# Prompt attention of a hybrid decoder step: rows of logits in a ring of six banks, one bank each for turned probabilities and values, and TensorE's program reordered

## The chip, the cores and the metric

The kernel runs on one core of a Trainium2 chip. The metric is the device time of one execution in microseconds (us), taken as the median of several executions.

## The reference, cut to what matters

One inference step of a one-layer decoder: RMSNorm, a combined input projection, a state-space branch, a sparse-attention branch, gates, an output projection and an MLP, for a prompt of 1024 positions and for 8 samples of 4 new tokens each. The change touches only the attention of the prompt, after its top-k mask is known:

```python
def attend_selected(q, k_sel, v_sel, sel_idx, q_pos, rel_bias):
    dist = q_pos[None, :, None] - sel_idx
    valid = dist >= 0
    bias = rel_bias.astype(jnp.float32)[t5_bucket(dist)]
    logits = jnp.einsum('bthd,btkhd->bthk', q, k_sel).astype(jnp.float32) * HEAD_DIM ** -0.5
    logits = logits + jnp.swapaxes(bias, -1, -2)
    logits = jnp.where(valid[:, :, None, :], logits, -jnp.inf)
    p = jax.nn.softmax(logits, axis=-1)
    return jnp.einsum('bthk,btkhd->bthd', p.astype(v_sel.dtype), v_sel)
```

There are 8 heads of 64 channels, 1024 prompt positions, and up to 256 keys selected for a position. The kernel does not gather the selected keys: it computes all logits up to the diagonal and hides the keys that were not selected with a mask.

## The kernel before, in words

The kernel is written by hand, engine by engine, in a row of blocks with a barrier between them; every wait is a semaphore. The block of the change is the prompt attention, whose engine programs start at line 1738 (SyncE) and 1766 (TensorE). Before it stand the projections, the indexer and the selection; after it come the attention of the samples, the output projection and the MLP.

**Tiles and pairs.** The prompt is cut into 8 tiles of 128 queries (i = 0 to 7). Tile i looks at `keys_of(i)` = 128 (i + 1) keys. Within a tile the heads go two at a time: pair u stands for (i, m), heads 2m and 2m + 1, called hh = 0 and 1. There are 32 pairs, and everything runs over them in order.

**What one pair costs on TensorE** (all in `@block.tensor`, from line 1766):
- *logits* (line 1781): q times k in fp32, 64 channels deep, so the two heads use the two row halves of the array at once; up to 512 keys go into one PSUM bank, so tiles 4 to 7 need two banks a head. Then the mask is added by a bf16 matmul (line 1787; tiles 0 and 1 only add the triangle, line 1789), and `qk_done` goes up for each head.
- *transposes* (line 1805): the probabilities (128 queries x 128 keys each) are turned, up to four into one bank. Such a set of up to four is a *group* (`groups`, `p_groups`); a head of tiles 4 to 7 has two of them.
- *values* (line 1823): for each block of 128 keys and each head one matmul of 64 columns, the two heads side by side in the column halves of the array, summed in the tile's values bank.
- *inverses* (line 1835), once a tile: the reciprocals of the row sums, spread over the channels, are turned so that they can multiply the result.

**The other engines.** VectorE adds the relative bias to the nearest 256 keys of a row in PSUM (line 1862) and takes the row's maximum (line 1867), in `row_max`; copies the turned groups of head 1 to SBUF (line 1876); forms the reciprocals (`invert`, lines 1882 and 1886); and multiplies the finished values by the turned reciprocals (`finish`, line 1892). ScalarE copies the turned groups of head 0 (line 1916), copies the turned reciprocals (`take_inverses`, line 1923) and computes the exponentials of a row from PSUM to SBUF with their sum (line 1932, each followed by the read of its accumulator). The copies go to a ring of 8 slots in SBUF (`PTs`). GpSimd and SyncE only prepare the next block: 32 small loads of bias, the value rows and pages of the samples' caches.

**The eight PSUM banks.** Banks 0 to 3 hold rows of logits (`row_bank`, line 1713): in tiles 0 to 3 one bank a row, so two pairs at a time; in tiles 4 to 7 two banks a row, so one pair. Banks 4 and 5 take the turned groups in turn (group g goes to bank 4 + g % 2, and waits until the copy of group g - 2 is done: `bank_free`). Banks 6 and 7 hold the values of an even and an odd tile.

**The order.** TensorE's program is a list written out by hand:

```python
            logits(0)
            for u, (i, m) in enumerate(PAIRS):
                if u + 1 < NPAIR:
                    logits(u + 1)
                transposes(u)
                if m == 1 and i:
                    inverses(i - 1)
                if u:
                    values(u - 1)
```

So each iteration u issues the logits of the next pair, turns the probabilities of this one and multiplies the values of the last. `logits(u)` waits, in tiles 4 to 7, for both exponentials of the pair before (its banks), in the others for those of two pairs before. VectorE's order is row_max(u + 1), at a new tile invert(i - 1), the copies of pair u, and in the third pair of a tile finish(i - 1). ScalarE's is the copies of pair u, in the second pair take_inverses(i - 1), then the exponentials of pair u + 1.

## Time and profile before

| | |
|---|---|
| median of 3 runs | 1810.75 us |
| lowest and highest | 1806.47 and 1811.78 us |
| span of the profiled execution | 1809.0 us |
| TensorE busy, share of the span | 1655.9 us, 92% |
| VectorE, ScalarE, GpSimd busy | 1153.2, 740.1, 704.3 us |
| attention block of the prompt | 681.2 to 845.0 us of the span |

The profile is one execution. Its page gives the span, from the first to the last instruction, and not that execution's own time; the span is 1.75 us under the median of the runs. Engine names in the rows: PE is TensorE's matmuls, PEld its weight loads, DVE VectorE, ACT ScalarE, POOL GpSimd, SP SyncE; L1805 is line 1805 of the kernel. A row of the order in time gives the start in us of the span, the time to the end of the last instruction merged in it, the engine, line and operation, out<-in with shapes, how many instructions it merges, and in brackets how long the engine had been idle and what released it. One fp32 matmul of products or values is recorded as two, and the two heads' matmuls start together. Ends of matmuls are modelled, so the text reckons from start to start. PEclk is the clock granted to TensorE: 1.00 is 2.4 GHz, 0.50 is 1.2 GHz.

### The profile page before, as it was taken

To read this page: it belongs to the slowest core of one execution; us is meant where nothing else is said; L and a number is where in the kernel's file an instruction comes from. 1 tells how busy PE (TensorE), PEld (TensorE's weight loads), DVE (VectorE), ACT (ScalarE), POOL (GpSimd) and SP (SyncE) were. 2 spreads that over 40 slices of the span, in tenths; PEclk is the share of its full clock that TensorE was granted. 3 is DMA by queue.
4 is the path that set the end of the run, shared out by engine and by line. 5 is a ranking of instruction groups with operands and counts; after the bars stand their busy time and mean duration, and the time that the engine had idled before them with its cause. 6 is when DMAs were issued, how large, how long until landed. Compare 5 with 4: busy or idle time off the path is not lost.

```text
span 1809.0 us, 31521 instructions
## 1 busy us (share of the span) xinstructions
PE 1655.9 (92%) x12434; PEld 1526.2 (84%) x12448; DVE 1153.2 (64%) x1860; ACT 740.1 (41%) x1337; POOL 704.3 (39%) x435
## 2 busy tenths in 40 slices
PE   6899869978999998788799999899999989999998
PEld 6798539978999875555399998899999989999998
DVE  5772557999866537655244138765555579989786
ACT  6323446556433525443322334534444433333342
POOL 7021105875211100000444431344444477777782
PEclk9999989998999998999899999999999989999999
DMA  6322161212853105002562443454544365444432
GB/s 159 114 64 48 28 77 51 91 60 87 148 123 122 54 19 189 1 1 75 172 216 96 125 125 95 146 192 142 176 152 143 143 243 167 155 155 143 138 90 97
DMA packets 170199, 209.13 MB, mean 116 GB/s; under 512 B 27411, under 2 KB 114419, under 8 KB 170003
## 3 DMA queue, kind: packets, MB, share of 16 engines
q1 hardware_dynamic: 170050, 207.10, 38.0%
q8 instruction: 99, 1.62, 0.4%
q14 instruction: 50, 0.40, 0.1%
HBM read 148.28 MB, written 58.78 MB: 114 GB/s over the span
## 4 chain that ended last, share of the span: by engine, by line
PE 29%; POOL 9%; DVE 4%; DMA 3%; issue 2%; ACT 2%; SPq 1%; DVEq 0%; ACTq 0%; POOLq 0%
PE psum L139 9%; PE psum L141 9%; PE psum L140 9%; POOL da_lo L3140 5%; DMA view_at<-hid_dram 3%; POOL view_at L3156 1%; POOL view_at L3149 1%; ACT da_hi L3016 1%; POOL view_at L3159 1%; POOL view_at L3152 1%; DVE view_at L3220 1%; SPq L2602 1%; DVE b_lo L3226 1%; DVE view_at L3351 0%; PE psum L2741 0%
## 5 line engine op out<-in xcount | busy, mean ns | idle before, releaser
L139 PE MATMUL psum<-db_hi,da_hi 128*128 128x264 f32 x896 | 257.0, 287 | 15.4 <-DVE view_at L3336 8.1
L139 PE MATMUL psum<-b_hi,ua_hi 128*128 128x264 f32 x896 | 256.4, 286 | 11.0 <-DVE psum L3284 3.8
L141 PE MATMUL psum<-db_hi,da_lo 128*128 128x264 f32 x896 | 256.6, 286 | 0.0
L140 PE MATMUL psum<-db_lo,da_hi 128*128 128x264 f32 x896 | 256.6, 286 | 0.0
L141 PE MATMUL psum<-b_hi,ua_lo 128*128 128x264 f32 x896 | 255.2, 285 | 0.0
L140 PE MATMUL psum<-b_lo,ua_hi 128*128 128x264 f32 x896 | 254.8, 284 | 0.0
L139 PE MATMUL psum<-h_hi,w_hi 128*128 128x352 f32 x600 | 198.4, 331 | 20.8 <-POOL w_lo L211 20.8
L3136 POOL TENSOR_TENSOR ua_lo<-view_at,ua_hi 128x512 fp32r<-128x512 f32 x99 | 137.3, 1391 | 189.1 <-ACT ua_hi L2945 189.0
L211 POOL TENSOR_TENSOR w_lo<-view_at,w_hi 128x2048 fp32r<-128x2048 f32 (+1 forms) x18 | 82.3, 4570 | 296.4 <-ACT w_hi L205 296.3
L140 PE MATMUL psum<-h_lo,w_hi 128*128 128x352 f32 x600 | 195.7, 326 | 0.0
L141 PE MATMUL psum<-h_hi,w_lo 128*128 128x352 f32 x600 | 195.5, 326 | 0.0
L139 PEld LDWEIGHTS psum<-db_hi,da_hi 128*128 128x128 f32 x896 | 170.4, 190 | 17.7 <-issue 8.3
L3140 POOL TENSOR_TENSOR da_lo<-view_at,da_hi 128x1024 fp32r<-128x1024 f32 x56 | 148.3, 2667 | 93.6 <-ACT da_hi L3016 93.6
L139 PEld LDWEIGHTS psum<-b_hi,ua_hi 128*128 128x128 f32 x896 | 169.2, 189 | 12.5 <-issue 11.5
L140 PEld LDWEIGHTS psum<-db_lo,da_hi 128*128 128x128 f32 x896 | 169.6, 189 | 0.0
L141 PEld LDWEIGHTS psum<-db_hi,da_lo 128*128 128x128 f32 x896 | 169.6, 189 | 0.0
L141 PEld LDWEIGHTS psum<-b_hi,ua_lo 128*128 128x128 f32 x896 | 169.4, 189 | 0.0
L140 PEld LDWEIGHTS psum<-b_lo,ua_hi 128*128 128x128 f32 x896 | 169.3, 189 | 0.0
L3351 DVE TENSOR_TENSOR view_at<-psum,view_at 128x528 f32<-128x528 f32 x204 | 134.6, 697 | 25.9 <-PE psum L141 23.4
L3315 DVE TENSOR_TENSOR db_lo<-view_at,db_hi 128x1056 fp32r<-128x1056 f32 x56 | 127.6, 2278 | 24.2 <-ACT db_hi L3011 24.0
L139 PEld LDWEIGHTS psum<-h_hi,w_hi 128*128 128x128 f32 x600 | 115.5, 193 | 23.0 <-issue 21.3
L139 PE MATMUL psum<-w_hi,h_hi 128*128 128x256 f32 x432 | 127.1, 294 | 3.0 <-PEq L1048 2.3
(394 smaller groups left out, 4061.6 us busy)
## 6 DMA issues: line engine op xcount, KB each, us to landing
hid_dram<-view_at SPq DMA_DIRECT2D x112, 264.0 KB, 2.3
view_at<-hid_dram SPq DMA_DIRECT2D x56, 528.0 KB, 3.8
view_at<-w_in SPq DMA_DIRECT2D x18, 1024.0 KB, 5.5
view_at<-w_up SPq DMA_DIRECT2D x16, 1024.0 KB, 6.0
view_at<-w_down SPq DMA_DIRECT2D x32, 512.0 KB, 5.6
gate_dram<-view_at SPq DMA_DIRECT2D x48, 176.0 KB, 2.0
view_at<-gate_dram SPq DMA_DIRECT2D x16, 528.0 KB, 4.5
view_at<-cache_k SPq DMA_DIRECT2D x32, 256.0 KB, 3.0
```

Of the source, the lines that this page charges most:

```text
L139: nc.tensor.matmul(out, lhs[0], rhs[0], start=start, stop=False, skip_group_check=more)
L140: nc.tensor.matmul(out, lhs[0], rhs[1], start=False, stop=False, skip_group_check=more)
L141: return nc.tensor.matmul(out, lhs[1], rhs[0], start=False, stop=stop, skip_group_check=more)
L211: nc.gpsimd.tensor_tensor(w_low[n % 2][:, :, 0:width], w_raw[n % 2][:, :, 0:width], f32(w_high[n % 2][:, :, 0:width]), ALU.subtract).then_ ...
L2602: sp.dma_start(raw_d[d % 2][:, k0::2, cols], w_dn[d][:, k0::2, cols]).then_inc(raw_d_in[j], 16)
L3016: nc.scalar.activation(dah[n % SLOTS], src_d(n), ACT.Copy).then_inc(da_hi, 1)
L3136: tt(slot_u(n)[1], src_u(n), f32(slot_u(n)[0]), ALU.subtract).then_inc(ua_lo, 1)
L3140: tt(dal[n % SLOTS], src_d(n), f32(dah[n % SLOTS]), ALU.subtract).then_inc(da_lo, 1)
L3149: tt(s_d[0], w21, w22, ALU.add).then_inc(sd_done, 1)
L3152: tt(s_d[1], s_d[0], w11, ALU.subtract).then_inc(sd_done, 1)
L3315: v.tensor_tensor(dbl[n % SLOTS], raw_b[n % 3], f32(dbh[n % SLOTS]), ALU.subtract).then_inc(db_lo, 1)
L3351: v.tensor_tensor(two(to), pair(mt), two(to), ALU.add).then_inc(drained, 1)
```

## The change

The banks are dealt out anew. Rows of logits get six banks as a ring: in tiles 0 to 3 (called narrow in the code) row n = 2u + hh goes to bank n % 6, three pairs at a time; in tiles 4 to 7 (wide) it goes to the two banks from 2 (n % 3), so three rows at a time. All turned groups go to bank 6, and each waits for the copy of the group before it. All values go to bank 7, and the first values of a tile wait until `finish` of the tile before is done.

In tiles 4 to 7 the copies are dealt out by key block and no longer by head: VectorE copies the first group of each head, ScalarE the second.

TensorE's program has a form for each kind of tile. The narrow one turns head 0 of pair u, issues the products of pair u + 2, turns head 1, adds the masks and multiplies the values of pair u - 1. The wide one splits the products of pair u + 1 into the first 512 keys and the rest, the values of pair u - 1 into three parts, and places them and the masks between the four groups that it turns. Products no longer wait for all exponentials of the pair ahead: in wide tiles for the first head's exponential of pair u - 1. The inverses move from the second pair of a tile to the end of the first, `finish` from the third to the second, `invert` from the start of the next tile to the fourth pair of its own. The orders of VectorE and ScalarE follow. No instruction that computes is added or taken away.

The diff, cut to its core (a line of "..." marks what is left out; every `psum[:, 4 + g % 2, ...]` becomes `psum[:, 6, ...]`, every `psum[..., 6 + i % 2, ...]` becomes `psum[..., 7, ...]`):

```diff
+    WIDE_ROWS = 4
+    U_WIDE = 4 * WIDE_ROWS
+    ON_ACT, ON_DVE = 0, 1
     groups = []
     p_groups = []
     inv_group = {}
     for u, (i, m) in enumerate(PAIRS):
-        p_groups.append(([], []))
+        p_groups.append([])
         for hh in range(2):
             for b0 in range(0, i + 1, 4):
-                p_groups[u][hh].append(len(groups))
-                groups.append((u, hh, b0, min(4, i + 1 - b0)))
-        if m == 1 and i:
+                eng = hh if i < WIDE_ROWS else (ON_ACT if b0 else ON_DVE)
+                p_groups[u].append(len(groups))
+                groups.append((u, hh, b0, min(4, i + 1 - b0), eng))
+        if m == 0 and i:
             inv_group[i - 1] = len(groups)
-            groups.append((u, 0, -1, 4))
+            groups.append((u, 0, -1, 4, ON_ACT))
     inv_group[NT - 2] = len(groups)
-    groups.append((NPAIR, 0, -1, 4))
-    def taken(g, hh):
-        return len([n for n in range(g + 1) if groups[n][1] == hh])
+    groups.append((NPAIR, 0, -1, 4, ON_ACT))
+    def taken(g, eng):
+        return len([n for n in range(g + 1) if groups[n][4] == eng])
...
+    def last_of(u, hh):
+        return [g for g in p_groups[u] if groups[g][1] == hh][-1]
+    def ahead(u):
+        if u < U_WIDE - 2:
+            return u + 2
+        return u + 1 if u > U_WIDE - 2 and u + 1 < NPAIR else None
...
-        return 2 * (u % 2) + hh if PAIRS[u][0] < 4 else 2 * hh
+        n = 2 * u + hh
+        return n % 6 if PAIRS[u][0] < WIDE_ROWS else 2 * (n % 3)
...
+            def products(u, spans):
                 i, m = PAIRS[u]
                 nk_ = keys_of(i)
-                if i >= 4:
+                if u > U_WIDE:
+                    pe.wait_ge(exp_done, 2 * u - 1)
+                elif u == U_WIDE:
                     pe.wait_ge(exp_done, 2 * u)
-                elif u >= 2:
-                    pe.wait_ge(exp_done, 2 * u - 2)
-                spans = [(n0, min(nk_, n0 + 512)) for n0 in range(0, nk_, 512)]
+                elif u >= 3:
+                    pe.wait_ge(exp_done, 2 * u - 4)
...
+            def hidden(u, hh):
+                i, m = PAIRS[u]
+                nk_ = keys_of(i)
+                for n0, n1 in spans_of(u):
+                    bank = psum[:, row_bank(u, hh) + n0 // 512, :]
+                    if i >= FIRST:
+                        last = mm(bank[:, 0:n1 - n0], hideb, mask_of(i)[:, n0:n1], start=False, stop=True)
+                    elif n1 == nk_:
+                        last = mm(bank[:, n1 - n0 - P:n1 - n0], identb, trib, start=False, stop=True)
+                last.then_inc(qk_done, 1)
...
+                if g:
+                    eng = groups[g - 1][4]
+                    pe.wait_ge(out_of[eng], taken(g - 1, eng))
+            def turn_p(u, n):
+                g = p_groups[u][n]
+                _, hh, b0, cnt_, _ = groups[g]
+                pe.wait_ge(exp_done, 2 * u + hh + 1)
+                bank_free(g)
+                for b in range(cnt_):
+                    last = tr(psum[:, 6, b * P:(b + 1) * P], Pb[:, hh, (b0 + b) * P:(b0 + b + 1) * P], ident)
+                last.then_inc(pT_done, 1)
...
+            def values(u, part, parts):
...
+                    if m == 0 and i:
+                        pe.wait_ge(y_done, i)
+                    for eng in (ON_ACT, ON_DVE):
+                        last_g = [g for g in p_groups[u] if groups[g][4] == eng][-1]
+                        pe.wait_ge(out_of[eng], taken(last_g, eng))
+                n = i + 1
+                cuts = (0, n) if parts == 1 else (0, n // 4, n // 4 + n // 2, n)
+                for j in range(cuts[part], cuts[part + 1]):
                     for hh in range(2):
                         h = 2 * m + hh
-                        g = p_groups[u][hh][j // 4]
-                        last = mm(psum[64 * hh:64 * hh + 64, 6 + i % 2, m * P:(m + 1) * P],
+                        g = [g for g in p_groups[u] if groups[g][1] == hh][j // 4]
+                        last = mm(psum[64 * hh:64 * hh + 64, 7, m * P:(m + 1) * P],
                                   vsb[:, j, h * HD:(h + 1) * HD], PTs[slot(g) % 8][:, j % 4, :],
                                   start=(j == 0), stop=(j == i))
-                last.then_inc(pv_done, 1)
+                        if hh and j == i:
+                            last.then_inc(pv_done, 1)
...
+            def narrow(u):
+                n = ahead(u)
+                turn_p(u, 0)
+                if n is not None:
+                    products(n, spans_of(n))
+                turn_p(u, 1)
+                if n is not None:
+                    hidden(n, 0)
+                    hidden(n, 1)
                 if u:
-                    values(u - 1)
+                    values(u - 1, 0, 1)
+                if PAIRS[u][1] == 0 and u:
+                    inverses(PAIRS[u][0] - 1)
+            def wide(u):
+                n = ahead(u)
+                if n is not None:
+                    products(n, spans_of(n)[0:1])
+                turn_p(u, 0)
+                if n is not None:
+                    products(n, spans_of(n)[1:2])
+                    hidden(n, 0)
+                turn_p(u, 1)
+                if n is not None:
+                    hidden(n, 1)
+                values(u - 1, 0, 3)
+                turn_p(u, 2)
+                values(u - 1, 1, 3)
+                turn_p(u, 3)
+                values(u - 1, 2, 3)
+                if PAIRS[u][1] == 0:
+                    inverses(PAIRS[u][0] - 1)
+            for u in range(2):
+                products(u, spans_of(u))
+                hidden(u, 0)
+                hidden(u, 1)
+            for u in range(U_WIDE):
+                narrow(u)
+            for u in range(U_WIDE, NPAIR):
+                wide(u)
             inverses(NT - 2)
-            values(NPAIR - 1)
+            values(NPAIR - 1, 0, 1)
...
-            row_max(0)
+            for u in range(2):
+                row_max(u, 0)
+                row_max(u, 1)
             for u, (i, m) in enumerate(PAIRS):
-                if u + 1 < NPAIR:
-                    row_max(u + 1)
-                if m == 0 and i:
-                    invert(i - 1)
-                evac(u)
-                if m == 2 and i:
+                n = ahead(u)
+                evac(u, 1 if i < WIDE_ROWS else 0)
+                if m == 1 and i:
                     finish(i - 1)
-            invert(NT - 2)
+                if n is not None:
+                    row_max(n, 0)
+                if i >= WIDE_ROWS:
+                    evac(u, 2)
+                if n is not None:
+                    row_max(n, 1)
+                if m == 3:
+                    invert(i)
             finish(NT - 2)
...
+            exps(0, 0)
+            exps(0, 1)
             for u, (i, m) in enumerate(PAIRS):
-                evac(u)
-                if m == 1 and i:
+                if i < WIDE_ROWS:
+                    evac(u, 0)
+                    exps(u + 1, 0)
+                    if u + 1 < U_WIDE:
+                        exps(u + 1, 1)
+                else:
+                    exps(u, 1)
+                    evac(u, 1)
+                    if u + 1 < NPAIR:
+                        exps(u + 1, 0)
+                    evac(u, 3)
+                if m == 0 and i:
                     take_inverses(i - 1)
-                if u + 1 < NPAIR:
-                    exps(u + 1)
             take_inverses(NT - 2)
```

## Rows read from the trace of the kernel before

**Rows 1.** table of windows: us from:to and length, busy us of each engine, clock, DMA

```profile
683.30:693.60 10.30, 8.99 (x45) 4.73 (x46) 5.56 (x20) 5.21 (x22) 0.98 (x5) 0.50 0.55 199
...
796.00:799.40 3.40, 3.40 (x30) 3.07 (x30) 0.00 (x0) 2.53 (x5) 0.00 (x0) 0.50 0.00 0
...
681.20:845.00 163.80, 137.43 (x1171) 91.71 (x1185) 103.20 (x201) 77.94 (x185) 2.87 (x10) 0.96 0.16 53
```

**Rows 2.** who waited for whom, 681.2 to 845: engine, line <- releaser, us, times, longest

```profile
PE psum L1805 <- ACT view_at L1916: 8.1, 16, 0.7
...
PE psum L1781 <- ACT view_at L1932: 7.3, 12, 1.3
...
PE psum L1835 <- DVE view_at L1876: 4.4, 4, 1.3
```

**Rows 3.** order in time, TensorE, the last two pairs of tile 7

```profile
829.98 1.99 PE L1781 MATMUL psum<-view_at,view_at 64*128 64x512 f32 x8 [0.98 <-ACT view_at L1932]
832.12 0.81 PE L1787 MATMUL psum<-view_at,view_at 128*128 128x512 bf16 x3 [0.16 <-issue]
832.77 1.04 PE L1805 MATMUL psum<-view_at,view_at 128*128 128x128 f32 x8
834.15 1.06 PE L1805 MATMUL psum<-view_at,view_at 128*128 128x128 f32 x8 [0.34 <-ACT view_at L1916]
...
837.04 1.09 PE L1805 MATMUL psum<-view_at,view_at 128*128 128x128 f32 x8
838.48 1.06 PE L1805 MATMUL psum<-view_at,view_at 128*128 128x128 f32 x8 [0.34 <-ACT view_at L1916]
839.47 1.97 PE L1823 MATMUL psum<-view_at,view_at 128*64 128x128 f32 x32
841.37 0.66 PE L1835 MATMUL psum<-view_at,view_at 128*128 128x128 f32 x4
841.95 1.97 PE L1823 MATMUL psum<-view_at,view_at 128*64 128x128 f32 x32
```

**Rows 4.** order in time, TensorE, starts of iterations in tiles 3 to 7

```profile
723.56 1.04 PE L1805 MATMUL psum<-view_at,view_at 128*128 128x128 f32 x8
...
731.86 0.70 PE L1781 MATMUL psum<-view_at,view_at 64*128 64x512 f32 x2 [1.32 <-ACT view_at L1932]
...
795.85 3.15 PE L1823 MATMUL psum<-view_at,view_at 128*64 128x128 f32 x28
...
812.79 1.99 PE L1781 MATMUL psum<-view_at,view_at 64*128 64x512 f32 x8 [0.34 <-ACT view_at L1932]
...
819.94 1.99 PE L1781 MATMUL psum<-view_at,view_at 64*128 64x512 f32 x8 [0.23 <-ACT view_at L1932]
```

**Rows 5.** order in time, VectorE and ScalarE, a pair of tile 7

```profile
832.54 0.43 DVE L1862 TENSOR_TENSOR psum<-psum,view_at 128x256 f32<-128x256 f32 x1 [5.55 <-PE psum L1787]
833.00 1.22 DVE L1867 TENSOR_REDUCE view_at<-psum 128x1 f32<-128x1024 f32 x1
...
836.94 0.68 DVE L1892 TENSOR_TENSOR view_at<-psum,view_at 128x512 f32<-128x512 f32 x1
...
833.41 1.09 ACT L1916 ACTIVATE view_at<-psum 128x512 f32<-128x512 f32 x2 [3.48 <-PE psum L1805]
834.38 1.12 ACT L1932 ACTIVATE view_at<-psum,view_at 128x1024 f32<-128x1024 f32 x1
835.37 0.21 ACT L1932 ACTIVATION_READ_ACCUMULATOR view_at<-psum,view_at 128x1 f32 x1
```

**Rows 6.** order in time, TensorE, tiles 0 to 3

```profile
686.87 0.69 PE L1823 MATMUL psum<-view_at,view_at 128*64 128x128 f32 x4 [1.17 <-DMA view_at<-out]
...
693.48 0.66 PE L1805 MATMUL psum<-view_at,view_at 128*128 128x128 f32 x4
...
714.38 1.13 PE L1781 MATMUL psum<-view_at,view_at 64*128 64x512 f32 x4
...
717.65 1.13 PE L1781 MATMUL psum<-view_at,view_at 64*128 64x512 f32 x4
```

More of the change, by code:

```diff
@@ L1782, in logits @@
                            start=True, stop=i < FIRST and n1 < nk_)
-                for hh in range(2):
-                    for n0, n1 in spans:
-                        bank = psum[:, row_bank(u, hh) + n0 // 512, :]
-                        if i >= FIRST:
-                            last = mm(bank[:, 0:n1 - n0], hideb, mask_of(i)[:, n0:n1], start=False, stop=True)
-                        elif n1 == nk_:
-                            last = mm(bank[:, n1 - n0 - P:n1 - n0], identb, trib, start=False, stop=True)
-                    last.then_inc(qk_done, 1)
@@ L1852, in _, with row_max @@
             v = nc.vector
-            def row_max(u):
+            def row_max(u, hh):
                 i, m = PAIRS[u]
```

113 lines of the change are left out of this document (44 added, 69 removed).

## The prediction

> **What bounds the kernel now.** I first read the table of windows for the stretch that the diff touches, the prompt attention block, then who waits for whom in it, then the order in time of TensorE, and last VectorE and ScalarE. The block runs from 681.2 to 845 us of the span: 163.8 us, of which TensorE is busy 137.4, VectorE 103.2, ScalarE 77.9 and the DMA engines 16% [rows 1]. Blocks before and after are separated from it by a barrier, the SP and GpSimd programs of the block aren't edited, and the loads it needs for values land once, early. So what the block gains or loses reaches the end one for one. TensorE's own order is the bound, and the waits inside it are what the change can take: 8.1 us in 16 pieces for ScalarE's copies out of the banks of turned probabilities, 7.3 us in 12 for exponentials before new products, 4.4 us in 4 before the turning of the inverses [rows 2]. A pair of tile 7 (1024 keys) takes 7.15 us from products to products in the plain case (812.79 to 819.94), and 10.04 us (to 829.98) for the iteration in which the inverses of the tile before are turned [rows 3, 4].
>
> **Prices, from start-to-start times at the full clock.** A turn (one 128x128 transpose) is 0.109 us: eight take 1.09, four 0.66 [rows 3]. Values cost 0.218 per key block of 128 (both heads): 839.47 to 841.37 is 8 x 0.218 plus 0.15 [rows 3]. Products: 512 keys 1.13, 1024 keys 1.99, so 0.43 per 256 keys, 0.214 per block [rows 3, 6]. The bf16 mask matmul is 0.215 per 512 keys, 0.108 per block for both heads [rows 3]. One block of keys costs TensorE 0.757 in all, 6.06 for a pair of tile 7, and the change alters none of it.
>
> What it alters is how often the array changes its tile form (64-row for products, 64-column for values, full for turns and masks). After the last matmul of one form the next form starts 0.09 to 0.10 late, and the first step of the new one is 0.05 longer (turns, values) or 0.10 (products). It is seen three times: turns to values 838.48 to 839.47 is 8 x 0.109 + 0.12, of which 0.03 is a restart; values to turns 0.15 as above; products 829.98 to 832.77 is 1.72 + 0.86 for the masks + 0.21 [rows 3]. Masks to turns costs nothing: 4 x 0.215 from 831.91 is 832.77 (the first of four isn't recorded) [rows 3]. So: into products 0.19, products to masks 0.10, products to turns 0.15 (not in the trace, its two halves are), values to turns 0.15, turns or masks to values 0.14. Check on before: 6.06 + 0.19 + 0.10 + 0.14 = 6.49, and 7.15 less that leaves 0.66 of waits, of which 0.34 stands in the row at 838.48 for the same wait of a bank [rows 3, 4]. For tile 3 the same sum is 3.03 less one values block 0.22, plus 0.43: 3.24, measured 3.27 from 714.38 to 717.65 [rows 6]. The prices hold.
>
> **Wide tiles (4 to 7), 15 iterations from the 17th pair's products.** The new order is products (first 512 keys), turn 0, products (rest), mask head 0, turn 1, mask head 1, values a, turn 2, values b, turn 3, values c. Nine changes of form in place of three: 0.19+0.15+0.19+0.10+0.14+0.15+0.14+0.15+0.14 = 1.35 against 0.43, so +0.92 per iteration. Tile 7: 6.06 + 1.35 = 7.41, if no wait is left. Is one left? A copy starts 0.31 after the last turn's start (833.10 to 833.41, the eight turns having begun at 832.77), and the bank is usable again 0.74 after that (833.41 to 834.15) [rows 3, 5]. One bank instead of two therefore means a turned group of four may follow the last by no less than 0.33 + 0.31 + 0.74 = 1.38. With t = 0 at the products: turn 0 at 1.05, turn 1 at 3.13, turn 2 at 4.66, turn 3 at 6.26, all further apart than 1.38. VectorE: masks of head 0 begin at 2.70, the bias add 0.63 later (831.91 to 832.54), 0.46 + 1.25 for add and maximum [rows 5] ends at 5.03; turn 2's copy wants VectorE at 5.35. Free, by 0.32. The exponential (1.2 with its accumulator [rows 5]) is done at 6.3, before 7.41 asks for it. No wait, period 7.41 against 7.15: plain pairs get slower.
> The gain is in the fourth pair of each tile. Before, turning the inverses waits for VectorE's copies behind two maxima, ScalarE's copy of them stands ahead of both exponentials, and the products wait for these: 10.04 - 7.15 = 2.89 [rows 3, 4]. After, they come at the end of an iteration whose products are already out: 0.436 + 0.15, and 0.27 for the bank in tile 7: 0.84, elsewhere 0.59.
> The same sums give periods of 5.58 (tile 4, with 0.17 + 0.27 of waits on the one bank, since its second product and turn 1 are short), 5.94 and 6.69. With the mixed pairs at the borders and 0.3 where the finish on VectorE delays tile 4: 23.2 + 24.5 + 27.5 + 22.9 = 98.0. Before: 731.86 to 837.04, 105.2 [rows 3, 4]. **-7.2.** Of it 1.6 is a fall of the granted clock to 1.2 GHz from 796.0 to 799.4, behind the idle at the inverses, which made values of 28 matmuls 3.15 long [rows 1, 4]; I take it as gone with that idle.
>
> **Narrow tiles (0 to 3).** Two products ahead rather than one. Form changes: values to turns, turns to products, products to turns, masks to values = 0.15+0.19+0.15+0.14 = 0.63 against 0.43, +0.2 per iteration, 10 of them from 693.48 to the turns of the 15th pair at 723.56 [rows 4, 6]. Before, that stretch is 30.1: 21.6 of matmuls (by the prices per block, tile by tile), 4.3 of form changes, 1.3 for three turned inverses and so 2.9 of waits; the ring takes these. But the inverses now stand just ahead of the next pair's first turn in the one bank, so each costs 1.4 (0.03 + 1.38): 21.6 + 6.4 + 3 x 1.4 = 32.2, or +2.1. At the start TensorE idles until the values land at 686.87 [rows 6]; one pair more of products fits ahead of it, -1.1 at 1.2 GHz (clock 0.50 from 683.3 to 693.6 [rows 1]), and two iterations at that clock cost 0.7 more: -0.4 net by 693.5, so narrow is +1.7 or +1.8; I take **+1.9** with rounding. The border into tile 4 is even: the next products wait for an exponential that starts only after the first wide row's masks, 8.4 from 723.56's turns against 8.3 [rows 4]: +0.1.
>
> **The end.** The last pair has no products to cover its four copies: turns at 0, 1.44, 2.84, 4.41, inverses at 5.85, last values at 6.4 for 1.7: 8.1, against 837.04 to 843.65, 6.6 [rows 3]. **+1.5.**
>
> **Moved at no cost:** finish, from the third pair to the second of a tile (0.68 on VectorE [rows 5], ahead of a maximum that has 0.3 to spare in tile 7; without that it costs the 0.3 counted for tile 4); inversion, from the next tile's first iteration to the last of its own (behind the maximum, VectorE idle after it); one values bank in place of two (its next use waits for the finish, done at 3.1 of an iteration that asks at 4.0). The count of instructions is unchanged, and no DMA moves.
>
> **Sum:** -7.2 + 1.9 + 0.1 + 1.5 = **-3.7 us**. The profiled execution has a span of 1809.0 us, 1.75 below the median of the runs shown, 1810.75, and what lies around the span isn't in the view; I carry the difference over: 1807.0. The measurement tells 0.3% (5.4 us) from nothing, no less.
>
> **Bounds.** Unknown is the price of a change of form between turns and products, and of one between such short pieces. Lowest from rows: nothing, as masks to turns, which makes 15 x 0.92 + 10 x 0.2 = 15.8 us less: 1791; a gain is excluded, since a change of form takes no work away. Highest: 0.24 each if it also restarts like a waited turn (0.03 more): 100 x 0.03 = 3 more. I take the rows of the same forms, 0.14 to 0.19.
>
> **Rivals.**
> *Cheap changes of form* (0.18). The late start of 0.09 stays, but with weights loaded ahead the long first step hides: 0.92 becomes 0.56 for 15 iterations, 0.2 becomes 0.1 for 10: -6.4, giving 1800.6. For: weight loads do run ahead within a form. Against: at each change in the trace they don't.
> The Trainium skill, in "TensorEngine Tiling (Array Packing)", Key Properties, says that a change of tiling mode drains TensorE, and "TensorE: Matmul & The Clock Gate", Part 2, puts a drain at about 128 cycles, so as an estimate 0.053 us at 2.4 GHz. With that alone the added changes would cost some 5 us and not 16, and the time would be near 1796; the trace agrees that there is a drain, but shows 0.14 to 0.19 for it and the refill.
> *The one bank becomes the chain* (0.10), the case on the other side. If VectorE ends the first head's maximum more than 0.5 later than I have it (0.32 of slack, and 0.17 before turn 3 asks), turn 2's copy waits for the maximum, turn 3 for the copy, and the values behind it. For: VectorE's order is fixed, copy, row, copy, row. Against: VectorE is busy 103 of 164 us [rows 1]. A maximum of 1.25 less the slack is 0.8 in each of 16 pairs: +12.8, 1819.8.
> *The clock fall stays or moves* (0.15). A wait that I missed is as long as the ones before 796, and 1.6 comes back: 1808.6.
> *The chain is as it was* (0.05). If new products still wait for both exponentials of the pair ahead, the ring buys nothing: 1810.7 to 1812.
>
> **How the numbers follow.** Forecast 0.52, 1807.0, its own range 1802 to 1812 (3 us of my sum, 3 us of the runs' scatter: 1806.5 to 1811.8). Over 0.3% faster is below 1805.3: nearly all of 0.18, a quarter of 0.52, a little of the clock case: 0.32. Over 0.3% slower, above 1816.2: 0.09. Within: 0.59. The range 1799 to 1814 leaves out the slow rival and the lower part of the cheap one.
>
> **What would show it.** Plain pairs of tile 7 at about 7.4 between products, no 10 us pair; waits of TensorE for ScalarE's copies near zero in tiles 5 to 7; the block near 160 us; in narrow tiles a wait of 0.8 behind each turned inverse; granted clock 1.00 from 732 on. Wrong if plain pairs of tile 7 take under 7.1 (changes of form cheap) or over 8 (bank chain), or if the block shrinks by over 8 us.

## The result, and the profile after

The changed kernel is slower. It took 1819.84 us in the median of 4 runs (1815.68 to 1821.01) where the kernel before took 1810.9 (1806.47 to 1811.78): ratio 1.0046, 95% interval 1.0027 to 1.0065. In a second set, 12 runs against 33, the ratio was 1.0031 (1.0017 to 1.0045). (One more run of the kernel before is left out of it: it took 1864.84 us at a mean granted clock of 0.867, where the others have 0.96 to 0.98.) The forecast of 1807.0 and its range up to 1814 are both missed, on the side to which I gave 0.09.

Lengths below are read the same way for each kernel. The **block** runs from the start of its first products to 1.7 us after the start of the last values. The **border** is the start of the products of pair 17, the second of tile 4 (731.86 before [rows 4], 740.95 after); pairs are counted from 0, as in the code. It cuts the block into a narrow part and a wide part with the end. Before: 681.28 to 731.86 to 843.65, so 50.6 + 111.8 = 162.4. After: 679.73 to 740.95 to 849.43, so 61.2 + 108.5 = 169.7. The spans differ by 4.9 (1813.9 against 1809.0), the medians by 8.9 and 6.8: the block's +7.3 is the whole of it, as near as scatter lets one say.

The table of windows of the changed kernel, for the stretch shown before, the stretch at half clock, and the wide tiles:

```profile
681.20:845.00 163.80, 150.52 (x1098) 85.57 (x1114) 106.94 (x195) 75.71 (x182) 1.43 (x7) 0.93 0.16 53
681.80:705.70 23.90, 21.91 (x98) 11.45 (x98) 13.33 (x40) 9.70 (x38) 0.95 (x5) 0.50 0.67 223
741.00:842.00 101.00, 96.88 (x749) 55.18 (x760) 67.90 (x104) 46.84 (x95) 0.00 (x0) 1.00 0.01 1
```

TensorE is busy 150.5 us where it was 137.4 [rows 1], with the same matmuls in the program (the stretch cuts 1.5 us off the start of the changed block and 4.4 off its end). Part of that is the clock: 1.2 GHz for 23.9 us at the block's start, where it was 10.2. The fall near 796 [rows 1] is gone, and the wide tiles run at 1.00 throughout.

Who waited for whom in it, TensorE's first rows:

```profile
PE psum L1850 <- DVE view_at L1951: 2.8, 3, 0.9
PE psum L1828 <- DVE view_at L1935: 2.6, 7, 0.9
PE psum L1828 <- ACT view_at L1988: 2.3, 3, 0.8
PE psum L1801 <- ACT view_at L1996: 1.3, 1, 1.3
PE psum L1828 <- ACT view_at L1981: 1.2, 3, 0.8
```

Of the 8.1, 7.3 and 4.4 us of [rows 2], 1.2, 1.3 and nothing are left (the fifth and the fourth row here). The new first row is one that I had priced at nothing: values (L1850) wait for `finish` (L1951), three times, in the narrow tiles. The third is the turned groups waiting for ScalarE's copy of the turned inverses (L1988), three times 0.78. The second is the one bank behind VectorE's copies: 0.88 us of it stands in the last pair, the rest in waits of at most 0.29.

TensorE in order of time in tile 3, with its waits:

```profile
727.83 0.63 PE L1828 MATMUL psum<-view_at,view_at 128*128 128x128 f32 x4 [0.78 <-ACT view_at L1988]
...
731.49 1.09 PE L1850 MATMUL psum<-view_at,view_at 128*64 128x128 f32 x16 [0.95 <-DVE view_at L1951]
...
733.94 0.63 PE L1828 MATMUL psum<-view_at,view_at 128*128 128x128 f32 x4 [0.78 <-ACT view_at L1981]
...
740.95 1.13 PE L1801 MATMUL psum<-view_at,view_at 64*128 64x512 f32 x4 [1.33 <-ACT view_at L1996]
```

The 0.78 at 733.94 belongs to pair 14, the one iteration without new products, where nothing stands between two groups turned into the one bank. VectorE in the iteration of the 0.95:

```profile
730.14 0.69 DVE L1935 COPY view_at<-psum 128x512 f32<-128x512 f32 x1 [2.06 <-PE psum L1828]
730.75 0.68 DVE L1951 TENSOR_TENSOR view_at<-psum,view_at 128x512 f32<-128x512 f32 x1
```

Here is the miss in two rows. `finish` had its inputs long before: the last values of tile 2 start at 725.59, and ScalarE's copy of the turned inverses released TensorE at 727.83. It stands behind VectorE's copy of the second head's turned group, for which VectorE sat idle 2.06 us. So it ends at 731.43, and the values, due 0.95 earlier, start at 731.49.

TensorE in the wide tiles: a pair of tile 7 with inverses, a plain one, and the last pair:

```profile
818.10 1.13 PE L1801 MATMUL psum<-view_at,view_at 64*128 64x512 f32 x4
...
825.50 0.66 PE L1863 MATMUL psum<-view_at,view_at 128*128 128x128 f32 x4
826.08 1.13 PE L1801 MATMUL psum<-view_at,view_at 64*128 64x512 f32 x4
...
833.57 1.13 PE L1801 MATMUL psum<-view_at,view_at 64*128 64x512 f32 x4
834.63 0.66 PE L1828 MATMUL psum<-view_at,view_at 128*128 128x128 f32 x4
835.21 1.13 PE L1801 MATMUL psum<-view_at,view_at 64*128 64x512 f32 x4
836.50 0.38 PE L1811 MATMUL psum<-view_at,view_at 128*128 128x512 bf16 x1 [0.16 <-issue]
836.72 0.60 PE L1828 MATMUL psum<-view_at,view_at 128*128 128x128 f32 x4
...
838.27 0.66 PE L1828 MATMUL psum<-view_at,view_at 128*128 128x128 f32 x4
...
839.88 0.66 PE L1828 MATMUL psum<-view_at,view_at 128*128 128x128 f32 x4
...
841.31 0.63 PE L1828 MATMUL psum<-view_at,view_at 128*128 128x128 f32 x4 [0.19 <-ACT view_at L1981]
842.81 0.63 PE L1828 MATMUL psum<-view_at,view_at 128*128 128x128 f32 x4 [0.88 <-DVE view_at L1935]
...
847.73 1.97 PE L1850 MATMUL psum<-view_at,view_at 128*64 128x128 f32 x32
```

With t = 0 at 833.57 the four turns start at 1.06, 3.15, 4.70 and 6.31, where the prediction had 1.05, 3.13, 4.66 and 6.26. A plain pair takes 7.49 (826.08 to 833.57) and one with inverses 7.98 (818.10 to 826.08), the latter in place of 10.04 [rows 3, 4]. The last pair takes 8.1 (841.31 to 849.43) in place of 6.6.

### The profile page after: what moved, and what is told of

It reads as the page before. It is cut to its first block, busy times and chain, and to the rows that moved or that the text cites. A ratio compares the mean times of both kernels' runs of the same rounds, so it can differ in the third digit from the quotient of the medians.

```text
span 1813.9 us, 31554 instructions
## 1 busy us (share of the span) xinstructions
PE 1674.5 (92%) x12434; PEld 1526.6 (84%) x12448; DVE 1153.9 (64%) x1860; ACT 741.9 (41%) x1337; POOL 696.8 (38%) x435
## 4 chain that ended last, share of the span: by engine, by line
PE 32%; POOL 8%; DVE 3%; DMA 3%; issue 2%; ACT 2%; SPq 1%; DVEq 0%; ACTq 0%; POOLq 0%
PE psum L139 10%; PE psum L141 10%; PE psum L140 10%; POOL da_lo L3213 4%; DMA view_at<-hid_dram 2%; POOL view_at L3222 1%; ACT da_hi L3089 1%; POOL view_at L3229 1%; POOL view_at L3232 1%; POOL view_at L3225 1%; SPq L2675 1%; DVE view_at L3293 0%; DVE view_at L3424 0%; PE psum L2814 0%; ACT db_hi L3084 0%
## 5 line engine op out<-in xcount | busy, mean ns | idle before, releaser
L139 PE MATMUL psum<-b_hi,ua_hi 128*128 128x264 f32 x896 | 256.8, 287 | 10.6 <-DVE psum L3357 3.8
L3209 POOL TENSOR_TENSOR ua_lo<-view_at,ua_hi 128x512 fp32r<-128x512 f32 x99 | 137.4, 1392 | 188.8 <-ACT ua_hi L3018 188.6
L139 PEld LDWEIGHTS psum<-b_hi,ua_hi 128*128 128x128 f32 x896 | 169.6, 189 | 12.1 <-issue 11.1
L141 PEld LDWEIGHTS psum<-b_hi,ua_lo 128*128 128x128 f32 x896 | 169.7, 189 | 0.0
L140 PEld LDWEIGHTS psum<-b_lo,ua_hi 128*128 128x128 f32 x896 | 169.6, 189 | 0.0
L3388 DVE TENSOR_TENSOR db_lo<-view_at,db_hi 128x1056 fp32r<-128x1056 f32 x56 | 121.0, 2161 | 15.5 <-ACT db_hi L3084 15.3
```

The source lines that it names most:

```text
L139: nc.tensor.matmul(out, lhs[0], rhs[0], start=start, stop=False, skip_group_check=more)
L140: nc.tensor.matmul(out, lhs[0], rhs[1], start=False, stop=False, skip_group_check=more)
L141: return nc.tensor.matmul(out, lhs[1], rhs[0], start=False, stop=stop, skip_group_check=more)
L3209: tt(slot_u(n)[1], src_u(n), f32(slot_u(n)[0]), ALU.subtract).then_inc(ua_lo, 1)
L3388: v.tensor_tensor(dbl[n % SLOTS], raw_b[n % 3], f32(dbh[n % SLOTS]), ALU.subtract).then_inc(db_lo, 1)
```

## The experiments

All at one glance. "Spell" is the time at half clock from the block's start to the border; each kernel was compared with the kernel before on its own chip.

| kernel | narrow | wide and end | block | spell | ratio, 95% interval |
|---|---|---|---|---|---|
| before | 50.6 | 111.8 | 162.4 | 10.2 | |
| before_again | 50.2 | 111.3 | 161.4 | 6.8 | 1.0007 (0.9994 to 1.0019) |
| before_fill | 48.2 | 111.3 | 159.5 | 0 | 0.9976 (0.9963 to 0.9988) |
| changed | 61.2 | 108.5 | 169.7 | 23.9 | 1.0046 (1.0027 to 1.0065) |
| after_again | 61.1 | 108.5 | 169.6 | 23.9 | 1.0031 (1.0017 to 1.0045) |
| few_forms | 61.1 | 108.3 | 169.5 | 23.9 | 1.0043 (1.0027 to 1.0060) |
| two_value_banks | 56.2 | 108.5 | 164.6 | 17.1 | 1.0010 (0.9995 to 1.0025) |
| after_fill | 61.8 | 108.5 | 170.3 | 17.1 | 1.0055 (1.0042 to 1.0068) |
| after_fill_early | 54.4 | 108.5 | 162.9 | 0 | 1.0006 (0.9992 to 1.0020) |
| two_banks_fill | 51.1 | 108.5 | 159.6 | 0 | 1.0008 (0.9992 to 1.0023) |
| hybrid | 50.5 | 108.5 | 158.9 | 10.2 | 0.9991 (0.9977 to 1.0006) |
| hybrid_two_parts | 50.4 | 106.6 | 157.0 | 10.2 | 0.9967 (0.9952 to 0.9982) |
| hybrid_fill | 48.3 | 108.5 | 156.8 | 0 | 0.9969 (0.9959 to 0.9979) |
| best | 48.0 | 105.0 | 153.0 | 0 | 0.9933 (0.9911 to 0.9955) |

A row's parts and spell come from the one profiled execution of that kernel, its ratio from all its runs. The wide part is so steady (108.5 in eight of these rows) that a tenth can be read in it. The ratio carries some 2 to 4 us of scatter, so single steps are read from the block, and the ratios say whether they arrive.

### before_again and after_again: how steady are the parts

No edit: the kernel before, and the changed one.

> The kernel before, once more, for its clock. In its first profile the granted clock was 0.50 for 10.2 us at the start of the attention block (683.3 to 693.6). If the length of that spell belongs to the order of the work, it is 10.2 again and the time is 1806 to 1812. If it is chance from one execution to the next, it is some other length, up to the 23.9 us of the changed kernel.

> The changed kernel, once more, for its clock and for a narrower interval. Its first profile had the clock at 0.50 from 681.8 to 705.7, 13.7 us longer than before. Theory A (the slow spell belongs to the new order of tiles 0 to 3): some 24 us again, and 1.005 of before. Theory B (the spell's length is chance): about 10 us in some executions, and times of both kinds, 1812 and 1820.

The 23.9 us at half clock and the 61 us of the narrow part are there again to 0.1. The kernel before shows that its own spell moves: 6.8 us from 689.4 on, and none near 796. That run gives the price of the fall near 796, with before_fill, which has none either: 111.3 in both against 111.8, so 0.5 us and not the 1.6 that I had given it. Those slow values [rows 4] mostly ran in time in which the products would have waited for the exponential anyway: in before_again the same values run at full speed, and the products behind them wait 0.99.

```profile
799.41 1.77 PE L1781 MATMUL psum<-view_at,view_at 64*128 64x512 f32 x8 [0.99 <-ACT view_at L1932]
```

### hybrid: which half of the change costs

Tiles 0 to 3 keep the order and the banks of before, tiles 4 to 7 have the new ones. The cut shows the ring and TensorE's narrow order; the banks of turned groups and values, the inverses and the orders of VectorE and ScalarE go back in the same way.

```diff
-        return n % 6 if PAIRS[u][0] < WIDE_ROWS else 2 * (n % 3)
+        return n % 4 if PAIRS[u][0] < WIDE_ROWS else 2 * ((n + 1) % 3)
...
-                turn_p(u, 0)
-                if n is not None:
-                    products(n, spans_of(n))
-                turn_p(u, 1)
+                products(u + 1, spans_of(u + 1))
+                hidden(u + 1, 0)
+                hidden(u + 1, 1)
+                turn_p(u, 0)
+                turn_p(u, 1)
```

> Tiles 0 to 3 in the order and banks of before, tiles 4 to 7 in those of the change. The changed profile puts +10.6 us into tiles 0 to 3 and the border, -4.9 into tiles 4 to 7 and +1.6 into the last pair. Theory A: the slow spell is 10.2 us again, the block is 159 us from the first products to the last values, and the time is 3.3 below before, 1807.5. If the loss sat in the wide tiles instead, it stays above 1815.

The narrow part is back at 50.5, the wide part stays at 108.5. So the wide order alone takes 3.3 us from 111.8, end included, and the narrow order alone puts 10.6 on. The half clock goes with the narrow order: 10.2 us again.

### few_forms: six changes of form in place of nine

In the changed kernel's wide tiles the products are one piece, both heads' masks follow one another, and the values come in two parts. That leaves six changes of form in a pair. Nothing is left out.

```diff
-                    products(n, spans_of(n)[0:1])
+                    products(n, spans_of(n))
                 turn_p(u, 0)
                 if n is not None:
-                    products(n, spans_of(n)[1:2])
                     hidden(n, 0)
+                    hidden(n, 1)
                 turn_p(u, 1)
-                if n is not None:
-                    hidden(n, 1)
-                values(u - 1, 0, 3)
+                values(u - 1, 0, 2)
                 turn_p(u, 2)
-                values(u - 1, 1, 3)
+                values(u - 1, 1, 2)
                 turn_p(u, 3)
-                values(u - 1, 2, 3)
```

> The changed kernel with one thing altered in tiles 4 to 7: products not split, both masks behind the first turned group, values in two parts. That is six changes of form in a pair instead of nine. By the prices in the prediction 0.43 less in each of 15 iterations, so a pair of tile 7 goes from 7.49 to 7.06 and the kernel is 6.5 us below the changed one, if the one bank still gets its 1.38 between groups. If changes of form cost nothing and waits set the period, it stays at 7.5.

A miss: the wide part is 108.3, 0.2 less. What the changes of form gave back, waits for the one bank took. TensorE's longest waits in this kernel's block:

```profile
PE psum L1828 <- DVE view_at L1932: 3.3, 10, 0.9
PE psum L1850 <- DVE view_at L1948: 3.0, 4, 0.9
PE psum L1863 <- ACT view_at L1978: 2.8, 5, 0.7
```

The first and the third are the one bank (L1828 and L1863 are turns, L1932 and L1978 the copies): with the pieces packed closer, groups ask for it before it is copied out, and in the iterations with inverses the copy is not hidden. From 741.4 on TensorE waits 5.4 us (2.2, 2.1, 0.8 for the bank, 0.3 for `finish`) where the changed kernel waits 1.9; the wait at the border and the gaps marked "issue" are left out of both. At least part of the rest is in waits that the view doesn't list. A plain pair of tile 7 (826.25 to 833.49) takes 7.24, so 0.25 less in place of 0.43, with no wait listed:

```profile
828.17 0.66 PE L1828 MATMUL psum<-view_at,view_at 128*128 128x128 f32 x4
828.88 0.81 PE L1811 MATMUL psum<-view_at,view_at 128*128 128x512 bf16 x3
829.71 0.63 PE L1828 MATMUL psum<-view_at,view_at 128*128 128x128 f32 x4
```

The three masks recorded from 828.88 take 3 x 0.215 and would let the second group start at 829.53. It starts at 829.71, which is 1.54 behind the first; in the last pair, where only the bank holds it, that distance behind a copy by VectorE is 1.50 (841.31 to 842.81 in the changed kernel). These 0.18 and the 0.25 make the 0.43. So the nine pieces aren't waste as a whole; they are what keeps the bank's turnaround covered.

### hybrid_two_parts: one change of form less

In the hybrid the values come in two parts and not three in the 12 wide pairs that turn no inverses. One of the nine changes of form goes, the one from the fourth group to the last values, 0.14 a pair (the products now follow turns and not values).

```diff
-                values(u - 1, 0, 3)
+                parts = 3 if PAIRS[u][1] == 0 else 2
+                values(u - 1, 0, parts)
```

> Tiles 0 to 3 as before, tiles 4 to 7 as changed, but values in two parts rather than three in the 12 pairs that turn no inverses: two changes of form fewer a pair. If a change of form costs the 0.14 to 0.15 seen before and the one bank still has its 1.38 between groups, a pair of tile 7 takes 7.49 less 0.29 plus the 0.15 of turns to products, 7.35, and tile 4 loses its 0.3 wait before turn 3: -2.5 us in the block against the kernel with three parts. If the third part was what covered the copy of turn 3, nothing is gained.

TensorE in the plain pair of tile 7:

```profile
814.01 1.13 PE L1810 MATMUL psum<-view_at,view_at 64*128 64x512 f32 x4
...
820.76 0.66 PE L1843 MATMUL psum<-view_at,view_at 128*128 128x128 f32 x4
821.35 1.13 PE L1810 MATMUL psum<-view_at,view_at 64*128 64x512 f32 x4
```

7.34 us (814.01 to 821.35) in place of 7.49, so 0.15 less where the price says 0.14. The wide part goes from 108.5 to 106.6, 1.9 less. By the price alone it would be 12 x 0.14 = 1.7; three waits of 0.29 for the bank in tile 4 go too, the wait ahead of the last pair grows from 0.19 to 0.78, and the last pair takes 0.2 more. The price of a form is real, since taking one away with no new wait gives it back; it isn't "cheap". Of the kernels so far this is the first whose ratio lies clear below one.

### two_value_banks: what the one bank for values costs

The changed kernel, but in tiles 0 to 3 the ring has five banks, and values use banks 5 and 7 in turn, so that they needn't wait for the `finish` of the tile just before. (With five banks the products wait for one exponential more.)

```diff
-        return n % 6 if PAIRS[u][0] < WIDE_ROWS else 2 * (n % 3)
+        return n % 5 if PAIRS[u][0] < WIDE_ROWS else 2 * (n % 3)
+    def v_bank(i):
+        return 5 if i < WIDE_ROWS and i % 2 == 0 else 7
...
-                    if m == 0 and i:
-                        pe.wait_ge(y_done, i)
+                    if m == 0 and i >= 2:
+                        pe.wait_ge(y_done, i if i >= WIDE_ROWS else i - 1)
```

> The changed kernel with a ring of five banks for rows in tiles 0 to 3 (the products of pair u + 2 stand behind turn 0, which has already waited for the exponential that frees the fifth) and two banks for values there, so the first values of a tile no longer wait for the finish of the one before. In the changed profile that wait was 0.9 us in each of tiles 1 to 3. Expected: those three waits gone, -2.8 us in the block. The spell at 1.2 GHz from 682 stays at 24 us if it belongs to the order of turns and products; if the waits themselves keep the clock down, it gets shorter and up to 7 us more go.

TensorE's waits for `finish` are gone (L1828 of the changed kernel is L1833 here); these stay:

```profile
PE psum L1833 <- DVE view_at L1940: 2.7, 7, 0.9
PE psum L1833 <- ACT view_at L1993: 2.3, 3, 0.8
```

The narrow part is 5.0 shorter, more than the 2.8 of the waits, but the spell is also 6.8 shorter here. This run alone can't share the 5.0 out between the two; two_banks_fill does. Nor does one profiled execution say whether the waits themselves had kept the clock down, since the kernel before moves its spell by 3.4 us without any edit.

### after_fill, after_fill_early, before_fill, hybrid_fill: what the half clock costs

Extra bf16 matmuls of 512 columns, whose results nothing reads. In after_fill 12 of them go into the bank of the coming products, two ahead of each of the products of pairs 2 to 7. In the other three there are 11, at places where TensorE waits anyway in the first pairs: all in bank 7, idle at that time, in before_fill and hybrid_fill; nine there and two in the bank of the coming products in after_fill_early, whose nine the cut shows.

```diff
+            def extra(k):
+                for _ in range(k):
+                    mm(psum[:, 7, :], hideb, mask_of(NT - 2)[:, 0:512], start=True, stop=True)
...
+                extra({0: 3, 1: 2}.get(u, 0))
                 turn_p(u, 0)
...
+                extra({1: 4}.get(u, 0))
                 if u:
                     values(u - 1, 0, 1)
```

> The changed kernel with two more bf16 matmuls of 512 columns ahead of the products of pairs 2 to 7, whose results the products overwrite: 12 of them, 2.6 us at 2.4 GHz, 5.2 at 1.2. Nothing else differs. Theory A (TensorE's clock stays at 1.2 GHz for 23.9 us because the new order feeds the array too little in tiles 0 and 1): the spell ends some 10 us earlier or never starts, which gives back 5 to 7 us against a cost of 3 to 4, so -2 to -3 net and a clock of 1.00 by 693. Theory B (the spell's end has nothing to do with what TensorE does there): still 23.9 us, and 5 us slower.

> Tiles 0 to 3 as before, tiles 4 to 7 as changed, and 11 extra bf16 matmuls of 512 columns into the idle values bank where TensorE waits anyway in the first four pairs (for the first exponentials, and for the load of the values). Theory A: the spell of 10.2 us at 1.2 GHz shortens or goes, up to -3 us. Theory B: it stays, and the extra matmuls cost 0 to 1 us.

> The changed kernel with 11 extra bf16 matmuls of 512 columns, 9 of them in the still idle values bank where TensorE waits in the first two pairs (three ahead of turn 0, two ahead of the second pair's, four ahead of the first values), and one ahead of the products of pairs 4 and 5. With the order of before the same matmuls removed the spell at 1.2 GHz altogether. Theory A: it goes here too, from 23.9 us to under 4, and the block from 169.7 us to 161 or 162, which is the clock's share of the loss (about 8 of 10.6 in tiles 0 to 3); the kernel is then equal to before, 1808 to 1810. Rival: waits and changes of form carry the loss, the spell goes and the block stays above 166.

> The kernel before with the same 11 extra matmuls, the change left out altogether. Theory A: its spell of 10.2 us at the block's start goes, the block shrinks by 2 to 3 us as it did under the changed wide tiles, and the kernel is 0.998 to 0.999 of before. Rival: the gain of 2 us seen with the extra matmuls needs the new wide tiles; here nothing.

The windows of, in this order, after_fill over its spell, hybrid_fill, after_fill_early and before_fill over their narrow parts:

```profile
682.80:699.90 17.10, 16.84 (x68) 7.46 (x66) 8.17 (x27) 6.14 (x27) 0.88 (x5) 0.50 0.54 186
```

```profile
681.20:729.50 48.30, 43.99 (x357) 26.30 (x357) 38.65 (x95) 30.21 (x88) 2.85 (x10) 1.00 0.54 177
```

```profile
681.00:735.40 54.40, 46.09 (x352) 26.17 (x357) 38.79 (x93) 29.07 (x86) 2.81 (x10) 1.00 0.46 157
```

```profile
683.00:731.20 48.20, 43.40 (x352) 26.18 (x356) 38.53 (x93) 30.26 (x88) 2.78 (x10) 1.00 0.54 178
```

after_fill came too late and on the path: its matmuls start as the clock falls (682.77, where the spell starts at 682.8), the spell is 17.1 long in place of 23.9, and the narrow part is 0.6 longer all the same. The early ones, in the waits, take the spell away altogether in each profiled execution (clock 1.00). That isolates the clock's price by order: changed kernel 61.2 to 54.4, **6.8**; hybrid 50.5 to 48.3, **2.2**; before 50.6 to 48.2, **2.4**. And what is left between new and old narrow order at full clock is 54.4 - 48.3 = **6.1** against hybrid_fill, 6.2 against before_fill, which no clock explains. Of the 10.6 us, some 4.5 (6.8 less 2.2 or 2.4) are thus the longer spell and 6.1 or 6.2 the order.

### two_banks_fill: the finish waits at full clock

after_fill_early with the edit of two_value_banks.

> The changed kernel with the eleven extra matmuls of after_fill_early (9 into the idle bank 7 in the first two pairs, one ahead of the products of pairs 4 and 5) and, in tiles 0 to 3, a ring of five banks for rows and two banks for values. Theory (the one bank for values costs tiles 0 to 3 three waits for finish of 0.94 us each, 2.8 us in all, whatever the clock): with the clock at full speed through the block the three waits go, and the block, 162.9 us in after_fill_early, is 160.0 to 160.3; ratio to the kernel before 0.999, against 1.0006 there. Rival (the waits only cover for others: the products or the turns behind them wait for the rows or the inverses instead): the block stays within 0.5 of 162.9 and the ratio at 1.0006. The other 6.1 less 2.8 us by which the new narrow order is behind the old at full clock should stay: first products to products of pair 17 in 51.6 us, against 54.4 there and 48.3 in hybrid_fill.

The block is 159.6 where it was 162.9, and the narrow part 51.1: 3.3 less, of which 2.9 are the three waits. The rival (the waits only cover for others) falls. The window:

```profile
683.60:734.60 51.00, 45.80 (x351) 26.15 (x355) 38.61 (x93) 29.35 (x86) 2.81 (x10) 1.00 0.49 168
```

The ratio didn't follow: 1.0008 against 1.0006 without the edit, where 3.3 us is 0.0018. Between these two the intervals, 0.0015 to both sides, leave room for it. But before_fill has the same block, 159.5, and a ratio of 0.9976 (0.9963 to 0.9988), which is clear of 1.0008 (0.9992 to 1.0023). So the 3.3 us are shown in the profiled execution and not in the time of this kernel, and the block of one execution doesn't tell the time to better than some 6 us (0.0032). The runs hold a hint: in before_fill, after_fill_early and hybrid_fill the granted clock, in the mean of all runs, is 0.0035 to 0.0038 above the kernel before on the same chip, and in two_banks_fill 0.0010. The clock may have fallen in executions of which there is no profile; that isn't shown.

### best: the parts that gain, together

The hybrid with two parts, the 11 early matmuls, and the last pair's turned groups and inverses dealt over banks 6, 4, 5, 6 and 4, which are free by then.

```diff
+        return {0: 6, 1: 4, 2: 5, 3: 6, 4: 4}[g - p_groups[NPAIR - 1][0]] if g >= p_groups[NPAIR - 1][0] else 6
```

> All that gained, together: tiles 0 to 3 in the order and banks of before, with the 11 extra matmuls; tiles 4 to 7 as changed with values in two parts where no inverses are turned; and the last pair's four groups and the last inverses turned into banks 6, 4, 5, 6, 4, since no more rows of logits need 4 and 5. The last pair took 8.2 us from its first turn to its last values against 6.6 before; with three banks 6.7. Expected block 156.9 less 2.1 less 1.5, 153.3 us against 162.4 before, and 0.9945 of before, 1800.5. If the parts take the same waits, it stops at 156 and 0.9965.

TensorE's last pair in it:

```profile
828.18 1.06 PE L1849 MATMUL psum<-view_at,view_at 128*128 128x128 f32 x8 [0.78 <-ACT view_at L2016]
829.17 1.09 PE L1871 MATMUL psum<-view_at,view_at 128*64 128x128 f32 x16
...
833.15 1.97 PE L1871 MATMUL psum<-view_at,view_at 128*64 128x128 f32 x32 [0.23 <-ACT view_at L2016]
```

Two groups are turned in one go (828.18, x8), and the pair takes 6.7 us (828.18 to 834.85) in place of 8.1; a wait of 0.78 ahead of it, 0.19 in the changed kernel, takes 0.6 of that back. The block is 153.0, the shortest, 9.4 under before, and the ratio 0.9933 (0.9911 to 0.9955), 6 runs: faster than the kernel before, and by the ratios than the changed one. The median difference to before, 10.3 us, agrees with the block.

## Why the prediction was wrong, point by point

**The step that failed** is the narrow tiles, "+1.9" with the border's "+0.1": measured +10.6. Cut as the prediction cut them, the start (to the turns of the 5th pair, pair 4 of the code) came out at 12.05 against 12.20, -0.15 where it had -0.4; the border (from the turns of the 15th pair, pair 14, on) at 8.44 against 8.30, the +0.1 that it had. The ten iterations between took 40.7 us (691.78 to 732.51) against 30.1, +10.65 where it had +2.1. The same ten at full clock, in after_fill_early and then in two_banks_fill:

```profile
690.87 0.41 PE L1831 MATMUL psum<-view_at,view_at 128*128 128x128 f32 x2
...
726.96 0.66 PE L1831 MATMUL psum<-view_at,view_at 128*128 128x128 f32 x4
```

```profile
693.22 0.41 PE L1836 MATMUL psum<-view_at,view_at 128*128 128x128 f32 x2
...
726.22 0.66 PE L1836 MATMUL psum<-view_at,view_at 128*128 128x128 f32 x4
```

These are 36.1 and 33.0, so the step failed in two terms.

- *"one values bank in place of two (its next use waits for the finish, done at 3.1 of an iteration that asks at 4.0)"*, priced at nothing. I timed that in a wide iteration and took it for all tiles. In a narrow one VectorE's copy of the second head, which `finish` stands behind, comes late in the iteration, and the values ask right after. Cost: 3 x 0.9 = 2.8 of waits in the profile after, 36.1 - 33.0 = 3.1 over the ten iterations.
- *"two iterations at that clock cost 0.7 more: -0.4 net by 693.5"*. I held the spell's end at 693.6 [rows 1] fixed. It moved to 705.7, and that is worth 40.7 - 36.1 = 4.6 in the ten iterations. Why the spell is longer stays open.

What is left, 33.0 - 30.1 = 2.9, stands against the 2.1 foreseen for changes of form and turned inverses. The wait of 0.8 behind each turned inverse is there as predicted, 0.78 three times. Of the last 0.8 us, 0.52 at full clock is a wait of the first turned inverses for VectorE's copy (693.28 in after_fill_early, 695.63 in two_banks_fill); the rest I can't place.

**Wide tiles, "-7.2"**: 740.95 to 841.31 is 100.4 against 105.2, so -4.8. The mechanism was right: no wait for an exponential after the border, no 10 us pair, waits near zero in tiles 5 to 7, nine changes of form that make plain pairs slower. A size was off. Plain pairs take 5.86 (747.20 to 753.06), 6.08 (771.42 to 777.50), 6.84 (797.26 to 804.10) and 7.49 (826.08 to 833.57) in tiles 4 to 7, products to products, against 5.58, 5.94, 6.69 and 7.41. With the pairs at the tiles' borders that makes 2.4 in all, inside the "100 x 0.03 = 3 more" that I kept as the upper bound; it is most where the pieces are shortest. The prices should have leaned to that end; which of the nine changes costs more than its row says isn't resolved.

**The end, "+1.5"**: 8.1 against 6.6, right.

**The rivals.** *Cheap changes of form* is refuted: plain pairs of tile 7 got slower, not faster, 7.49 against 7.15, and hybrid_two_parts got 0.15 back in a plain pair of tile 7 for one change less. By the rule of the Trainium skill ("TensorEngine Tiling (Array Packing)", Key Properties) there is a drain, and the trace agrees that changes cost, 0.14 to 0.19 us each by the prices that held; the estimate of 0.053 us from 128 cycles was too low for the whole of it. *The one bank becomes the chain*: not in the changed kernel's wide tiles, whose waits for it are 0.29 and only up to 769.90, but few_forms shows that it lies close behind. Its forecast, 1819.8, meets the measured 1819.84 by accident, from another place. *The clock fall stays or moves*: it did move, to the block's start and not into the wide tiles, and a price of 1.6 was given to the wrong fall: that one was worth 0.5, the longer spell 4.6.

**The sum, corrected:** -4.8 wide, +10.6 narrow and border, +1.5 end = +7.3, as the block shows. None of my cases had the narrow tiles as the loser, and 0.09 for slower was far too little: two kinds of iteration had been changed, and I had walked the queues of one.

## What to carry to other kernels

When a change takes a buffer away, walk the last reader of that buffer through its engine's queue in every kind of iteration, the short ones first: a step that costs 0.7 us and is ready early still arrives late if it stands behind a copy that isn't. When a new order puts short pieces where TensorE's clock is down, don't keep the spell's old end; and look first whether idle TensorE time ahead of the spell can be filled. Judge a two-part change by its parts: here one half was worth -3.3 us and the other +10.6, and the half that gains, with the extra matmuls, one change of form less and the spread last pair, gave 0.9933.

Not tried: `finish` ahead of VectorE's copy in the second pair of a narrow tile. By the rows of tile 3 its inputs are ready at about 728 (the inverses' copy releases TensorE at 727.83) and VectorE is idle until 730.14, so the one bank for values should then cost nothing; it is an argument from rows and not shown.

## What was not expected of the hardware

TensorE stayed at 1.2 GHz while it was nearly always busy by the profile: 21.91 of 23.90 us in the changed kernel, and all 6.80 of 6.80 in before_again:

```profile
689.40:696.20 6.80, 6.80 (x34) 3.45 (x32) 5.10 (x16) 3.97 (x15) 0.00 (x0) 0.50 0.13 38
```

The work there is short: turns of one or two blocks, products of 128 or 256 keys, masks. Eleven further matmuls, 2.4 us of work at full clock (11 x 0.215 [rows 3]), kept the clock at 1.00 over the whole narrow part in the profiled executions of three kernels, and shortened the block by 2.1 (hybrid), 2.9 (before, 0.5 of it the fall near 796) and 6.8 us (changed). The busy time of the profile thus doesn't tell the two levels apart here; what does, these runs don't show. The Trainium skill ("TensorE: Matmul & The Clock Gate", Part 4) says that a transpose does not count as busy TensorE in the same way for the clock. The spell in a stretch full of turns fits that, but products and masks ran in it too, and the turns of the wide tiles, 16 of 0.109 us in a pair of tile 7, run at 1.00. No run here separates them.
